# Loading every second weight unit of a mixture-of-experts layer from ScalarE's hardware queue

## The reference

```python
def moe_swiglu(h, router_w, w1, w3, w2):
    t = h.reshape(-1, shp[-1])
    logits = (t @ router_w).astype(jnp.float32)
    top_v, top_i = lax.top_k(logits, TOP_K)
    ...
    for e in range(N_EXPERTS):
        y = y + gates[:, e:e + 1] * swiglu(t, w1[e], w3[e], w2[e])
```

## Time and profile before

| | |
|---|---|
| median of 3 runs | 1982.29 us (1981.83 to 1983.09) |
| profiled execution, span | 1983.4 us, 1.1 us above that median |
| granted TensorE clock, mean | 0.956 |
| busy: PE, DVE, ACT | 1852.7 us (93%), 1370.8 us (69%), 1127.1 us (57%) |
| bytes read | 475.5 MB, 240 GB/s over the span |
| expert weights on SP's queue | 672 issues of 512 KB |

### The profile page before, as it was taken

How to read it: one execution, slowest core, us unless ns; L and a number is a source line. 1 busy time by engine, 2 the same in 40 slices (tenths; PEclk the granted TensorE clock), 3 DMA queues, 4 the chain that set the end, 5 groups by cost and what they waited for, 6 DMA issues and landing times.

```text
span 1983.4 us, 25850 instructions
## 1 busy us (share of the span) xinstructions
PE 1852.7 (93%) x8533; PEld 1468.1 (74%) x8533; DVE 1370.8 (69%) x1651; ACT 1127.1 (57%) x1488; POOL 18.6 (1%) x37
## 2 busy tenths in 40 slices
PE   5898889899999979977999999999999999999996
PEld 1786447788888867746888888888888888888884
DVE  1444665434333456366878999989999999999995
ACT  2322343422222244244677778887888778887784
POOL 1000000000000000000000000000000000000000
PEclk7899989999999979987899999999999999999997
DMA  9431882332323314174698999999999999999991
GB/s 312 144 100 54 297 312 75 96 100 94 102 89 102 95 56 139 53 275 169 235 350 295 352 372 321 374 347 351 371 322 373 351 343 374 326 370 353 344 370 70
DMA packets 228106, 477.57 MB, mean 241 GB/s; under 512 B 14968, under 2 KB 37648, under 8 KB 228032
## 3 DMA queue, kind: packets, MB, share of 16 engines
q1 hardware_dynamic: 225920, 470.42, 66.7%
q0 software_dynamic: 2112, 6.20, 1.3%
HBM read 475.51 MB, written 1.05 MB: 240 GB/s over the span
## 4 chain that ended last, share of the span: by engine, by line
PE 87%; DVE 6%; ACT 3%; issue 2%; DMA 2%; SPq 0%; DVEq 0%; ACTq 0%; POOL 0%
PE ps L424 26%; PE ps L426 25%; PE ps L425 25%; PE ps L450 2%; PE ps L669 2%; PE ps L728 1%; DMA raw<-in_ada_w 1%; PE ps L699 1%; DMA pg_bc<-in_post_ffn_g 1%; PE ps L544 1%; DVE w_lo L1081 1%; PE ps L465 1%; DVE att L1278 0%; PE ps L557 0%; PE ps L474 0%
## 5 line engine op out<-in xcount | busy, mean ns | idle before, releaser
L1081 DVE TENSOR_TENSOR w_lo<-raw,w_hi 128x1024 fp32r<-128x1024 f32 x570 | 684.4, 1222 | 298.9 <-ACT w_hi L814 261.8
L1006 ACT ACTIVATE w_hi<-raw 128x1024 fp32r<-128x1024 f32 x448 | 473.1, 1061 | 109.1 <-PE ps L426 109.1
L424 PE MATMUL ps<-w_hi,he_hi 128*128 128x512 f32 x896 | 355.9, 397 | 3.0 <-DVE w_lo L1081 2.5
L426 PE MATMUL ps<-w_hi,he_lo 128*128 128x512 f32 x896 | 350.7, 391 | 0.0
L425 PE MATMUL ps<-w_lo,he_hi 128*128 128x512 f32 x896 | 350.0, 391 | 0.0
L1081 DVE TENSOR_TENSOR w_lo<-raw_more,w_hi 128x1024 fp32r<-128x1024 f32 x224 | 272.4, 1224 | 32.5 <-ACT w_hi L1006 14.3
L1006 ACT ACTIVATE w_hi<-raw_more 128x1024 fp32r<-128x1024 f32 x224 | 237.6, 1063 | 65.0 <-PE ps L426 65.0
L814 ACT ACTIVATE w_hi<-raw 128x1024 fp32r<-128x1024 f32 x122 | 129.1, 1063 | 241.7 <-PE ps L426 241.7
L424 PEld LDWEIGHTS ps<-w_hi,he_hi 128*128 128x128 f32 x896 | 169.1, 189 | 40.2 <-DVE w_lo L1081 5.8
L426 PEld LDWEIGHTS ps<-w_hi,he_lo 128*128 128x128 f32 x896 | 168.8, 188 | 36.3
L425 PEld LDWEIGHTS ps<-w_lo,he_hi 128*128 128x128 f32 x896 | 169.1, 189 | 33.8
(11 more groups left out here) (215 smaller groups left out, 2201.0 us busy)
## 6 DMA issues: line engine op xcount, KB each, us to landing
raw<-in_moe_w SPq DMA_DIRECT2D x448, 512.0 KB, 5.4
raw_more<-in_moe_w SPq DMA_DIRECT2D x224, 512.0 KB, 5.3
raw<-in_ada_w SPq DMA_DIRECT2D x96, 512.0 KB, 7.0
raw<-in_ffn_w SPq DMA_DIRECT2D x66, 512.0 KB, 3.5
raw<-in_w_in SPq DMA_DIRECT2D x40, 512.0 KB, 3.6
raw<-in_w_out SPq DMA_DIRECT2D x16, 512.0 KB, 8.9
ab_bc<-in_ada_b POOLq DMA_DIRECT2D x8, 256.0 KB, 4.5
xs<-in_x SPq DMA_DIRECT2D x2, 512.0 KB, 7.6
```

The lines of the kernel that those rows point to most:

```text
L424: pe.matmul(o, lh, rh, start=start, stop=False)
L426: return pe.matmul(o, ll, rh, start=False, stop=stop)
L1006: act.activation(w_hi[:, s % SPL, :], expert_raw(i), ACT.Copy).then_inc(hi_done, 1)
L1081: dve.tensor_tensor(w_lo[:, s_ % SPL, :], src, w_hi[:, s_ % SPL, :].bitcast(F32), ALU.subtract)\
```

## The change

Units with an odd number are loaded by ACT instead of SP. `expert_load(queue, e, i, base)` is the issue that stood in SP's loop, with the queue as an argument. SP skips the odd units, except for the first twelve units of expert 0. ACT issues the load of unit i + 8 (`ahead = i - SPL + RAW_E`) when i is odd, behind its two waits and ahead of its ACTIVATE for unit i; past the end of an expert it is a unit of the next one. The raw buffer that it fills is that of unit i - 4, so the wait for `unit_used` covers it. SP's loop now begins at expert 1, with expert 0 written out; ACT's loop covers experts 1 to 6, with experts 0 and 7 written out.

```diff
+        def expert_load(queue, e, i, base):
+
+            w, s, n = expert_units()[i]
+            if w == 2:
+                src, dst = moe_w2[0][e][n * P:(n + 1) * P, :], expert_raw(i)
+            else:
+                wt = moe_w1 if w == 0 else moe_w3
+                src = wt[0][e][2 * n * P:2 * (n + 1) * P, 512 * s:512 * s + 512].rearrange("(k p) n -> p k n", p=P)
+                dst = expert_raw(i).rearrange("p (k n) -> p k n", k=2)
+            queue.dma_start(dst, src).then_inc(expert_in(i)[0], 16)
...
             def experts(turn):
                 base = turn * NE * UE
-                with sp.Fori(0, NE) as e:
-                    for i, (w, s, n) in enumerate(expert_units()):
-
-                        sp.wait_ge(lo_done, e * UE + (NS0 + base + i - RAW_E + 1))
...
+                def expert(e, first):
+                    for i in range(UE):
+                        if i % 2 == 0 or first and i < RAW_E:
+                            sp.wait_ge(lo_done, e * UE + (NS0 + base + i - RAW_E + 1))
+                            expert_load(sp, e, i, base)
+
+                expert(0, True)
+                with sp.Fori(1, NE) as e:
+                    expert(e, False)
...
-            def split_expert_unit(i, e, base):
+            def split_expert_unit(i, e, base, first, last):
                 s = NS0 + base + i
                 landed, count = expert_in(base + i)
                 act.wait_ge(landed, e * (16 * UE // RAW_E) + count)
                 act.wait_ge(unit_used, e * UE + (s - SPL + 1))
+                ahead = i - SPL + RAW_E
+                if ahead % 2 and ahead < UE and not (first and ahead < RAW_E):
+                    expert_load(act, e, ahead, base)
+                if ahead % 2 and ahead >= UE and not last:
+                    expert_load(act, e + 1, ahead - UE, base)
                 act.activation(w_hi[:, s % SPL, :], expert_raw(i), ACT.Copy).then_inc(hi_done, 1)
...
-                expert(0, True)
+                expert(0, True, False)
...
-                with act.Fori(1, NE) as e:
-                    expert(e, False)
+                with act.Fori(1, NE - 1) as e:
+                    expert(e, False, False)
+                expert(NE - 1, False, True)
```

More of the change, by code:

```diff
@@ L1010, in experts, with expert @@
                 modulate(2 * (NE + 1) * turn)
-                def expert(e, first):
+                def expert(e, first, last):
                     done = [AHEAD + 1 if first and turn == 0 else 0]
@@ L1016, in split_to @@
                         for i in range(done[0], min(i1, UE - 1) + 1):
-                            split_expert_unit(i, e, base)
+                            split_expert_unit(i, e, base, first, last)
                         done[0] = max(done[0], i1 + 1)
@@ L1054, in _ @@
             for i in range(AHEAD + 1):
-                split_expert_unit(i, 0, 0)
+                split_expert_unit(i, 0, 0, True, False)
             act.wait_ge(sg("gap"), NLAT)
```

## The result

The changed kernel takes 1992.25 us (median of 8 executions, 1988.14 to 1994.78), the kernel before 1984.78 us in 8 executions (1981.83 to 1989.70). The ratio is 1.0036, 95% interval 1.0024 to 1.0048: slower by 4.8 to 9.5 us. The three executions of before that were known first lay at the low end of its scatter. The forecast's sign was right and its size was not: it added 4.2 us, and its range ended at 1991.0.

What follows compares the result with a forecast made beforehand. PE was taken to bound the experts, with one hole at each expert boundary; seven boundaries x 0.60 us = 4.2 us, all else nothing, added to the median 1982.29 gave 1986.5 us, 0.21% slower; range 1983.0 to 1991.0.

Steps and rivals of the forecast that it cites:

- The forecast's sign: Whole kernel: slower, by 4.2 us or 0.21%.
- The boundary term: Between experts: ACT issues unit 11's load before unit 3's hi part, delaying PE's restart; 7 x 0.60 = 4.2 us.
- Rival A: Boundary: address and MOVE made before the wait ends, only the DMA costs; 7 x 0.42 = 2.9 us, 1985.2; chance 0.30.
- "Cost nothing" in mid-step: Within steps of an expert: odd units 0.6 us late, absorbed by PE's slack of 1.05 to about 1.7 us.
- Rival C: ACT's issues cost 1 us or more, or collide with SP's; 7 us and up, 1989.5 to 1993; chance 0.10.
- D: DMA engines: two queues move less, loads land 10 us after issue instead of 5.3; some 2030 us; chance 0.04.
- ACT's loop stays loaded: ACT's expert loop: no instructions read again at jumps back, though it grows from some 230 to 340; cost nothing.
- rival B: ACT's loop of 340 instructions reads again at five jumps back; 2.5 to 12 us on top, 1989 to 1998.5; chance 0.10.
- "Nothing there lies on a chain by more than tenths": Expert 0, where ACT issues from unit 5 on: no issue delays a chain by more than tenths of a us.

Runs made afterwards that it cites:

- Experiment 7: Kernel with ACT's experts written out and all 84 loads per expert on ACT (SP only expert 0's first twelve), against the kernel before: 1987.91 us, ratio 1.0020.
- experiment 6: Changed kernel, loop kept, with ACT loading only units 3, 7, 11, ... (21 per expert) and SP the rest; against the kernel before: 1986.30 us, ratio 1.0013.
- experiment 3: Changed kernel with ACT's experts 1 to 6 written out instead of a hardware loop; against the kernel before: 1987.52 us, ratio 1.0019.
- Experiment 2: Kernel before, no load moved, with two idle waits behind every unit in ACT's expert loop: 1999.18 us against 1983.99, ratio 1.0076.
- experiment 8: Changed kernel with ACT loading only unit 11 of experts 1 to 7, all other loads on SP; against the kernel before: ratio 1.0002.
- the second profile: The unaltered changed kernel run once more for another profile: that execution took 1988.51 us.
- experiment 9: Changed kernel with ACT's experts written out and every odd unit but 11 loaded by ACT; against the kernel before: ratio 0.9998.
- experiment 5: Changed kernel with its loop kept and the issue moved behind the ACTIVATE of its unit; against the kernel before: 1987.72 us, ratio 1.0022.

## Why the prediction missed

**The boundary term was right.** Forecast 0.60 us by the sum of SP's rows; measured 0.56 to 0.62 in the loop and 0.47 to 0.48 where the expert is written out and the address instruction falls away. It was forecast for seven boundaries, 4.2 us in all; measured 3.8 with one load moved, 3.1 to 3.4 written out. Rival A's 0.42 was too low, even without the address instruction.

**"Cost nothing" in mid-step was right.** Experiment 7 has an issue before every unit and PE loses nothing in any of the 49 steps from expert 1 on. The timeline after shows how it is absorbed: PE releases ACT, the issue takes 0.36 us at 1347.78, the ACTIVATE starts at 1348.19, and PE is still behind. Rival C's dear issue falls, but for the first one: 0.33 to 0.41 us each on ACT, as on SP, with two of 0.45 and 0.46 in the first profile. So does D: landing is 5.3 to 5.5 us in the median in the changed kernel, the loads of ACT's queue among them, and no row shows ACT waiting for data. (In experiment 6 it was 6.5 on SP's queue and 7.0 on ACT's, and cost nothing either.)

**The step that failed is that ACT's loop stays loaded.** The sum put this at nothing, and rival B, which denied it, had 0.10. The runs show that the loop of 345 instructions doesn't stay loaded: ACT stops at each of five jumps back, and with the loop written out (experiment 3) 3.4 of the 7.2 us are gone. The chance of 0.10 rested on SP's loop of 306 instructions that reads nothing again, and on the hope that 345 is near enough. Experiment 2 shows that 317 on ACT is already too much. The three rows of evidence that were there (233, 206 and 306 recorded instructions, no stop) said nothing about 345, so a chance of about a half would have been fair.

B's mechanism held, and its sum only in part. It forecast 340 instructions, and 345 are recorded. It forecast a read of 3.4 us or more at each jump, which would cost 0.5 to 2.4 us; measured are stops of 2.7 to 3.9 us, and 0.0 to 1.1 at unit 0. It added this to the 4.2 us in full, but the two share one cover, so that between the experts the stops added 1.7 us in the first profile and nothing in the second, against experiment 8 with its 3.8. The result, 1992.25, lies inside B's 1989 to 1998.5 with the help of terms that B didn't have: the first issue, the stop behind the experts, and the higher median of the kernel before.

A stop behind a branch stood in the trace of before, and the forecast passed over it. Behind the experts ACT jumps over a second turn that this input doesn't need, and the chain there shows (start, us, what):

```profile
1969.80 0.05 ACTq L1060
1969.85 3.13 issue
```

All fourteen profiles have it, with 2.6 to 3.6 us. It is a jump forward, so it says nothing on whether the loop stays loaded, but its size is near that of the stops at the jumps back, 2.7 to 3.9 us.

By the rule of the Trainium skill (Runtime: NRT & Kernel Launch, "Instruction fetch mechanics") the sequencer of an engine other than PE holds two blocks of 256 instructions, and a taken branch out of them waits for a read. By that a body longer than one block fits only if it lies across no more than two. These runs agree, though none was made to test the place: 303 on ACT has no stop and 317 has, with the same code ahead of them; and the length alone can't be the rule, for SP's loop of 306 has no stop in the kernel before, while in experiment 8 one of 303, with 85 more recorded instructions ahead of it, has one of 4.4 to 5.2 us:

```profile
L389 SPq COMPARE_BRANCH  x1: 45/45/45, 1435.3 to 1435.3; - x1
L389 SPq FUSED_REGOPS  x1: 55/55/55, 1440.5 to 1440.5; - x1
```

**"Nothing there lies on a chain by more than tenths" was wrong for expert 0.** ACT's first issue is longer than the others. In the changed kernel its row reads:

```profile
L312 ACTq DMA_DIRECT2D raw_more<-in_moe_w x1: 1222/1222/1222, 955.2 to 955.2; - x1
```

Behind it PE reaches unit 7 0.82 us later, in both profiles; where the first issue took 0.43 us (experiments 3 and 9) the loss was about 0.33. In experiment 5 the first issue took 1.05 us, behind the ACTIVATE, and PE lost nothing at these units.

**The account.** For the first profile: expert 0 began 1.3 us earlier and gained 0.2 more at its unit 2; then it lost 0.8 us by the long first issue and some 1.2 by the clock of that execution; experts 1 to 7 lost 5.5, of which 3.7 are what the second profile has too and 1.8 the longer stops; behind the last unit 0.6 were lost, 1.7 by the stop there less 1.1 that other pieces took less time. That is 6.6 us, the difference of the spans. Without what belongs to one execution, the traces give the change a price of 6.1 us (0.8 + 3.7 + 1.6) with short stops and 8.0 (0.8 + 5.5 + 1.7) with long ones; the timed executions say 4.8 to 9.5. How long the stops are in executions without a trace can't be seen. And 2.5 us of the miss in absolute time are the base: 1982.29 was the median of three executions, 1984.78 of eight. From that base the forecast's 4.2 us alone would have given 1989.0, inside the range.

## What to carry to other kernels

Before adding instructions to a hardware loop, count those that the profile records per round on that engine; a loop that is known to stay loaded at one length and place says nothing about a longer or shifted one. At a jump back that reads again, find how long the engines behind can live on what is buffered (here 2.75 us): below it the stop is free, above it every microsecond is paid. A DMA issue on a compute engine costs its 0.5 to 0.6 us only where that engine is the next link of a chain, so a single issue in 84 may carry the whole price: put it behind the ACTIVATE that others wait for, and keep the queue's first issue away from a tight place. Look behind the loop as well: here lines that the change didn't touch got a stop of 1.6 us or more on the chain to the end.

## What the runs showed that was not expected

The stop at a jump back has no fixed length: 2.4 to 2.6 us in experiment 5, 2.7 to 3.9 in the changed kernel, 4.3 to 5.9 in experiment 2 with a shorter body, 4.4 to 5.2 on SP in experiment 8. SP's cost PE nothing, since twelve raw buffers lie behind it.

The first load that ACT's queue issues took 0.43 us in six profiles, 1.05, 1.18 and 1.22 in three, all of kernels whose loop has the full 42 issues (the same three that stop behind the experts), and 4.12 in one that was written out; why it is long is not settled.
